# Two rows of a three-product matmul in one instruction of 512 columns, in the feed-forward and pool input blocks

## The reference, cut to what matters

```python
f = rms_norm(h, g_ffn_pre[l])
f = jnp.square(jax.nn.relu(f @ w_ff1[l])) @ w_ff2[l]
h = h + rms_norm(f, g_ffn_post[l])
...
h = _rmsnorm(x, pre_g) * (1 + scale) + shift
proj = h @ w_in
y = _multiscale_pool(proj[..., :POOL_WIDTH], pool_w, pool_scale) * jax.nn.silu(proj[..., POOL_WIDTH:])
x = x + gate * _rmsnorm(y @ w_out, post_g)
```

## Time and profile before

| | |
|---|---|
| median of 3 runs | 1908.66 us (1908.66 to 1909.58) |
| the profiled execution | 1913.2 us, its span 1911.5 us |
| mean granted clock of PE | 0.985 |
| PE busy | 1840.2 us, 11620 matmuls |
| PE weight loads busy | 1663.0 us |
| DVE busy | 1437.2 us |
| ACT busy | 885.8 us |
| POOL busy | 117.3 us |
| HBM read | 419.14 MB, 221 GB/s over the span |

### The profile page before, as it was taken

The page is one execution under the profiler, slowest core; times in us unless marked ns, Lnnn a source line. Parts: engine busy times, 40 slices in busy tenths (PEclk is TensorE's granted clock), DMA queues, the critical chain, the costliest instruction groups (busy, mean ns, idle before and its releaser), DMA issues.

```text
span 1911.5 us, 29730 instructions
## 1 busy us (share of the span) xinstructions
PE 1840.2 (96%) x11620; PEld 1663.0 (87%) x11620; DVE 1437.2 (75%) x1655; ACT 885.8 (46%) x1146; POOL 117.3 (6%) x217
## 2 busy tenths in 40 slices
PE   6999999999999999999999979998999998999997
PEld 6999978799889988998998868887888787999976
DVE  4799986777777798887888978654677577786854
ACT  5344556454434433443344456423566445444442
POOL 0100000100110000000000000001110000000000
PEclk9999999999999999999999989999999998999998
DMA  7865435957898787777777655644443684778652
GB/s 261 290 193 191 162 134 209 327 163 271 309 311 278 241 279 257 251 248 260 251 260 284 237 202 195 209 170 154 153 146 130 234 282 132 240 227 273 210 176 89
DMA packets 185319, 424.80 MB, mean 222 GB/s; under 512 B 8192, under 2 KB 8576, under 8 KB 183680
## 3 DMA queue, kind: packets, MB, share of 16 engines
q1 hardware_dynamic: 157568, 322.69, 49.7%
q0 software_dynamic: 27648, 100.68, 15.8%
HBM read 419.14 MB, written 4.19 MB: 221 GB/s over the span
## 4 chain that ended last, share of the span: by engine, by line
PE 88%; DVE 7%; DMA 2%; ACT 2%; issue 1%; SPq 0%; DVEq 0%; POOLq 0%; POOL 0%; ACTq 0%
PE acc L1743 13%; PE acc L1744 13%; PE acc L1745 13%; PE acc L1756 13%; PE acc L1757 13%; PE acc L1758 13%; DVE mod_sum L1199 2%; PE aux L1794 2%; DVE w_lo L1010 2%; PE aux L2008 1%; DMA mod_raw<-in_ev_mod_w 1%; PE aux L2024 1%; PE aux L1999 1%; PE acc L2024 1%; PE aux L1758 1%
## 5 line engine op out<-in xcount | busy, mean ns | idle before, releaser
L495 ACT ACTIVATE w_hi<-raw 128x1024 fp32r<-128x1024 f32 x552 | 578.3, 1057 | 720.8 <-PE acc L1745 347.7
L1010 DVE TENSOR_TENSOR w_lo<-raw,w_hi 128x1024 fp32r<-128x1024 f32 x552 | 667.5, 1223 | 265.9 <-ACT w_hi L495 264.3
L1743 PE MATMUL acc<-a_hi,w_hi 128*128 128x256 f32 x2304 | 659.5, 286 | 3.6 <-DVE w_lo L1010 3.2
L1745 PE MATMUL acc<-a_hi,w_lo 128*128 128x256 f32 x2304 | 653.4, 284 | 0.0
L1744 PE MATMUL acc<-a_lo,w_hi 128*128 128x256 f32 x2304 | 653.3, 284 | 0.0
L1743 PEld LDWEIGHTS acc<-a_hi,w_hi 128*128 128x128 f32 x2304 | 443.4, 192 | 5.4 <-DVE w_lo L1010 3.6
L1744 PEld LDWEIGHTS acc<-a_lo,w_hi 128*128 128x128 f32 x2304 | 443.4, 192 | 0.7 <-issue 0.5
L1745 PEld LDWEIGHTS acc<-a_hi,w_lo 128*128 128x128 f32 x2304 | 443.1, 192 | 0.0
L1049 DVE SCALAR_TENSOR_TENSOR mod_sum<-mod_raw,silu_c,mod_sum 128x1024 f32<-128x1024 f32 x240 | 301.4, 1279 | 25.6 <-DMA mod_raw<-in_ev_mod_w 16.2
L1756 PE MATMUL acc<-w_hi,b_hi 128*128 128x512 f32 x768 | 302.0, 393 | 0.0
L1757 PE MATMUL acc<-w_lo,b_hi 128*128 128x512 f32 x768 | 300.0, 391 | 0.0
(11 more groups left out here) (217 smaller groups left out, 1437.8 us busy)
## 6 DMA issues: line engine op xcount, KB each, us to landing
raw<-in_w_ff SPq DMA_DIRECT2D x128, 1024.0 KB, 6.7
mod_raw<-in_ev_mod_w POOLq DMA_DIRECT2D x96, 512.0 KB, 5.1
mod_raw<-in_od_mod_w POOLq DMA_DIRECT2D x96, 512.0 KB, 5.2
raw<-in_w_in SPq DMA_DIRECT2D x40, 1024.0 KB, 5.2
raw<-in_ev_w_in SPq DMA_DIRECT2D x40, 1024.0 KB, 5.2
raw<-in_od_w_in SPq DMA_DIRECT2D x32, 1024.0 KB, 5.6
raw<-in_w_out SPq DMA_DIRECT2D x16, 1024.0 KB, 5.2
raw<-in_ev_w_out SPq DMA_DIRECT2D x16, 1024.0 KB, 6.3
```

The lines of the kernel that those rows point to most:

```text
L495: nc.scalar.activation(w_hi[:, s % SLOTS], raw[:, s // 2, KPS * (s % 2):KPS * (s % 2) + KPS, :], ACT.Copy).then_inc(hi_ready, 1)
L1010: nc.vector.tensor_tensor(w_lo[:, s % SLOTS], raw[:, s // 2, KPS * (s % 2):KPS * (s % 2) + KPS, :], w_hi[:, s % SLOTS].bitcast(F32), ALU.s ...
L1743: nc.tensor.matmul(o, wh, hi[:, k, :], start=first and t == 0 and f % 2 == 0, stop=False, skip_group_check=True)
L1745: last = nc.tensor.matmul(o, wl, hi[:, k, :], start=False, stop=t == KPS - 1, skip_group_check=True)
```

## The change

`a_hi` and `a_lo` become the halves of one tensor `a_pair`. `wide_step` does high and low rows in one matmul with the high weights, 512 columns into one bank, and then low weights x high rows, 256 columns into the bank's second half. A 512-column block takes four banks: hidden blocks, `odu` and `odg` use banks 0 to 3 and 4 to 7 in turn; outer blocks take two banks of the eight each. The halves are added on reading: ACT copies the low halves into `hid`, `u_low` or `silu_g`, DVE adds the high halves from PSUM. The relu, and the silu of the gate, then read the sum. `b_lo` of a hidden block is made in the next block's first place. `sum_mod` of od_shift and ev_shift moves behind step 3 of groups 2 and 3, and PE's loops over feed-forward blocks are written out. The spread of the modulation's halves is new, and so are `gate_steps`. On POOL the loads of od_scale for row tiles 7 and 8 go behind `stage_q(0, 0)`. The diff, cut (ACT and DVE runs of `split_hi` move step 4 of a block behind the low copy):

```diff
-        a_hi = sb("a_hi", [P, KT, T], F32R)
-        a_lo = sb("a_lo", [P, KT, T], F32R)
+        a_pair = sb("a_pair", [P, 2, KT, T], F32R)
+        a_hi, a_lo = a_pair[:, 0], a_pair[:, 1]
...
-        acc = [ctx.enter_context(nc.psum_tensor(f"acc{i}", [P, 1024], F32)) for i in range(2)]
-        aux = ctx.enter_context(nc.psum_tensor("aux", [P, 4, 512], F32))
+        banks = ctx.enter_context(nc.psum_tensor("banks", [P, 8, 512], F32))
+        aux = banks[:, 4:8, :]
+        two_banks = [banks[:, 2 * i:2 * i + 2, :].rearrange("p a n -> p (a n)") for i in range(4)]
+        acc = two_banks[:2]
+        wide_acc = [banks[:, 0:4, :], aux]
+        wide_high = [w[:, :, 0:T] for w in wide_acc]
+        wide_low = [w[:, :, T:2 * T] for w in wide_acc]
+        def outer_acc(g, bi):
+            return two_banks[bi if g < FF_GROUPS - 1 or bi < 3 else 0]
...
-            load_mod("od_scale", "od", 1, 1, KT // 2 + 1)
+            load_mod("od_scale", "od", 1, 1, KT // 2 - 1)
...
             pool.wait_ge(q_T_ready, 5)
             stage_q(0, 0)
+            load_mod("od_scale", "od", 1, KT // 2 - 1, KT // 2 + 1)
...
+                    n = 4 * g + bi
                     if b > BLOCK["ff"]:
-                        split_hi(b, range(4, 8))
+                        split_hi(b, range(4 if bi == 0 else 5, 8))
                     split_hi(b + 1, range(4))
-                    act.wait_ge(acc_free, 2 + ACC["ff"] + 8 * g + bi + 1)
+                    block_done(b)
+                    if n:
+                        act.wait_ge(hid_ready, n)
+                    nc.scalar.activation(hid, wide_low[bi % 2], ACT.Copy).then_inc(low_out, 1)
+                    split_hi(b + 1, [4])
+                    act.wait_ge(relu_ready, n + 1)
                     nc.scalar.activation(hid, relu, ACT.Square).then_inc(hid_sq, 1)
                     nc.scalar.activation(b_hi[:, 4 * bi:4 * bi + FT, :], relu, ACT.Square).then_inc(hid_hi, 1)
...
-            def spread(p, start, num, den, first, last):
-
-                done = lambda q: min(max(first + (q - start) * num // den, first), last)
+            def spread(p, start, end, total, hidden=1, outer=1):
+                weight = lambda places: sum(hidden if q // 8 % 8 < 4 else outer for q in places)
+                done = lambda q: total * weight(range(start, q)) // weight(range(start, end))
                 return done(p), done(p + 1) - done(p)
...
-                        halves("ev_shift", *spread(p, 80, 5, 12, 0, 32))
...
-                        halves("od_shift", *spread(p, 23, 5, 8, 0, 32))
...
+                        halves("od_shift", *spread(p, 22, 70, 32))
...
+                        halves("ev_shift", *spread(p, 75, 155, 32, 3, 4))
...
+            def hidden_low(n):
+                bi = n % 4
+                dve.wait_ge(hid_hi, n + 1)
+                nc.vector.tensor_tensor(b_lo[:, FT * bi:FT * (bi + 1), :], hid,
+                                        b_hi[:, FT * bi:FT * (bi + 1), :].bitcast(F32), ALU.subtract).then_inc(hid_ready, 1)
+            def ff_beside(g, block):
+                mods = ff_mods(8 * g + block)
+                def go(i):
+                    if i == 0 and 1 <= block <= 4:
+                        hidden_low(4 * g + block - 1)
+                    mods(i)
+                return go
             def ff_hidden(g):
 
                 for bi in range(4):
-                    each_ahead(BLOCK["ff"] + 8 * g + bi, ff_mods(8 * g + bi), 8, 0 if g or bi else 4)
-                    block_done(BLOCK["ff"] + 8 * g + bi)
-                    if not (g or bi):
+                    n = 4 * g + bi
+                    each_ahead(BLOCK["ff"] + 8 * g + bi, ff_beside(g, bi), 8, 0 if n else 4)
+                    dve.wait_ge(low_out, n + 1)
+                    nc.vector.tensor_tensor(relu, wide_high[bi % 2], hid, ALU.add).then_inc(acc_free, 1)
+                    if n == 0:
                         dve.wait_ge(rstd_ready, 1)
-                    nc.vector.scalar_tensor_tensor(relu, acc[bi % 2][:, :].rearrange("p (f t) -> p f t", f=FT), 0.0, rstd_b,
-                                                   ALU.max, ALU.mult).then_inc(acc_free, 1)
-                    dve.wait_ge(hid_hi, 4 * g + bi + 1)
-                    nc.vector.tensor_tensor(b_lo[:, FT * bi:FT * (bi + 1), :], hid,
-                                            b_hi[:, FT * bi:FT * (bi + 1), :].bitcast(F32), ALU.subtract).then_inc(hid_ready, 1)
+                    dve.wait_ge(acc_free, 2 + ACC["ff"] + 8 * g + bi + 1)
+                    nc.vector.scalar_tensor_tensor(relu, relu, 0.0, rstd_b, ALU.max, ALU.mult).then_inc(relu_ready, 1)
...
-                product = acc[bi % 2][:, :].rearrange("p (t n) -> p t n", t=TT)
+                product = outer_acc(g, bi).rearrange("p (t n) -> p t n", t=TT)
...
+                        dve.wait_ge(low_out, 4 * FF_GROUPS + g + 1)
+                        e = nc.vector.tensor_tensor(u_pad[:, :, POOL_PAD:POOL_PAD + T], wide_high[g % 2], u_low, ALU.add)
+                        e.then_inc(acc_free, 1)
...
-            gate_steps = [(1, 0, 1, 0)] * 5 + [(1, 1, 1, 1)] * 2 + [(2, 2, 0, 0)]
+            def gate_sum(n):
+                dve.wait_ge(low_out, 4 * FF_GROUPS + 4 + n + 1)
+                g4 = silu_g[:, FT * n:FT * (n + 1), :]
+                nc.vector.tensor_tensor(g4, wide_high[n % 2], g4, ALU.add).then_inc(g_summed, 1)
+                dve.sem_inc(acc_free, 1)
+            gate_steps = [(1, 1, 1, 0)] * 2 + [(1, 0, 1, 0)] * 2 + [(0, 0, 0, 0)] + [(1, 1, 1, 1)] * 2 + [(2, 2, 0, 0)]
...
-            dve.wait_ge(acc_free, 2 + ACC["pool"])
             for g in range(4):
+                if g == 0:
+                    gate_sum(3)
+                dve.wait_ge(silu_done, g + 1)
...
+            def wide_step(b, s, rows, out):
+                for t in range(KPS):
+                    k = KPS * s + t
+                    for f in range(FT):
+                        wh = w_hi[:, s % SLOTS, t, P * f:P * (f + 1)]
+                        wl = w_lo[:, s % SLOTS, t, P * f:P * (f + 1)]
+                        nc.tensor.matmul(out[:, f, :], wh, rows[:, :, k, :], start=s == 0 and t == 0, stop=False,
+                                         skip_group_check=True)
+                        last = nc.tensor.matmul(out[:, f, T:2 * T], wl, rows[:, 0, k, :], start=False,
+                                                stop=s == STEPS - 1 and t == KPS - 1, skip_group_check=True)
+                return last
+            def wide_product(b, a, region, beside=None):
+                pe.wait_ge(acc_free, a + 1)
+                for s in range(STEPS):
+                    pe.wait_ge(split_done, 8 * b + s + 9)
+                    wide_step(b, s, a_pair, wide_acc[region]).then_inc(step_done, 1)
+                    if beside:
+                        beside(s)
...
+            for g, unit in ((2, "od_shift"), (3, "ev_shift")):
+                def sum_beside(s):
+                    if s == 3:
+                        pe.wait_ge(acc_free, 2 + ACC["ff"] + 8 * g)
+                        sum_mod(unit, 2, g - 2)
+                wide_product(BLOCK["ff"] + 8 * g, ACC["ff"] + 8 * g, 0, sum_beside)
+                pe.wait_ge(mod_cols_ready, g - 1)
+                ff_hidden(g, 1)
+                ff_outer(g, 4 * g, g == FF_GROUPS - 1)
+            sum_mod("ev_scale", 2, 2)
...
-                nc.scalar.activation(silu_g[:, FT * n:FT * (n + 1), :], acc[n % 2][:, :].rearrange("p (f t) -> p f t", f=FT),
-                                     ACT.Silu).then_inc(acc_free, 1)
+                nc.scalar.activation(silu_g[:, FT * n:FT * (n + 1), :], wide_low[n % 2], ACT.Copy).then_inc(low_out, 1)
...
+            def g_silu(n):
+                act.wait_ge(g_summed, n + 1)
+                g4 = silu_g[:, FT * n:FT * (n + 1), :]
+                nc.scalar.activation(g4, g4, ACT.Silu).then_inc(silu_done, 1)
```

114 lines of the change are left out of this document (63 added, 51 removed).

## The result

| | before | after |
|---|---|---|
| median of the runs | 1909.06 us (1908.66 to 1913.25, 5 runs) | 1899.2 us (1890.78 to 1901.72, 5 runs) |
| profiled execution | 1913.2 us, span 1911.5 | 1895.4 us, span 1893.7 |

A forecast was written before the change was run, and what follows sets the result against it. It took PE to be bound by columns plus 13.3 ns a matmul. 20.5 (matmuls) + 8.1 (queue edit) - 1.4 (pool block) - 1.0 (loads) = 26.2 us, so 1882.5 us; range 1876 to 1898.

The forecast's parts named there:

- Columns plus 13.3 ns a matmul: PE's price in feed-forward: its columns plus 13.3 ns for each matmul at any width; only the second can be saved.
- the 20.5: Gain in us from 64 fewer matmuls in each of 24 blocks (16 hidden, 4 odu, 4 odg), 0.853 us a block.
- the seam: Wide matmul's two 256-column runs, 16 KB apart: taken as free; rival: 13.3 ns, no matmul gain, 1902 us, chance 0.08.
- Added work at nothing: Feed-forward blocks: added ACT and DVE work fits beside PE, DVE at 19.3 of 22.19 us hidden, 20.3 of 21.77 outer.
- Modulation loads in the feed-forward part: Denser od_shift loads: margin falls from 0.8 to 0.25 us a buffer turn; cost 0 to 18.6 us, taken as 1.
- Rival (a): Modulation loads set the pace in the denser feed-forward stretch: 7.4 us lost, 1890 us, at worst 1901; chance 0.13.
- The queue edit: POOL, second attention: od_scale loads behind stage_q(0, 0) end PE's wait ahead of head 0; 8.1 us gained, bounds 5.4 to 8.2.
- Rival (d): Second attention: the stage copy doesn't free PE, since something else ends last there; gain 18.1 us, 1890.5 us; chance 0.09.
- The pool block: Gate adds on DVE in the last odg block and later modulation loads delay the chain behind: 1.4 us lost.
- a stall of 1.5 us at the second pool group: Sign in the pool block: PE stalls since bank 2 is now freed by the gate add; inside the 1.4 us.
- Rival (e): Feed-forward pairs: the 256-column matmul waits for the wide one to drain, 0.163 us a pair, 2133 us; chance 0.04.
- Rival (c): Matmul saving is only that of the skill's figure, something else makes the 13.3 ns: gain 9.5 us, 1899 us; chance 0.04.

The follow-up runs named there:

- the run with one contiguous run: Changed kernel with a_pair laid out so the 512-column matmul reads one run of 512 columns, not two of 256: 1899.56 us, ratio 0.9936.
- the unchanged kernel: The changed kernel run once more with nothing edited, against the kernel before: 1901.49 us, ratio 0.9943.
- the kernel with eight and eight first: Mended kernel with eight wide, then eight narrow matmuls in the first step of every 512-column block: 1892.14 us, ratio 0.9895.
- The mended kernel: Changed kernel with gate halves beside pool input as before, and block 29's transfers ahead of SP's wait for the last hidden tile: 1891.41 us, ratio 0.9907.
- four and four first: Mended kernel with four wide, four narrow, four wide, four narrow matmuls in the first step of every 512-column block: 1886.22 us, ratio 0.9868.

## Why the prediction was wrong

**Columns plus 13.3 ns a matmul.** It held for matmuls of one length in a row, and the alternation reaches it only in one of two patterns. 226.7 + 120 = 346.7 ns is seen, in the pool input blocks of the profiled run; in 15 of the 16 feed-forward hidden blocks it was 353.3. That is the first failed step: 15 x 0.43 = 6.4 us of the 20.5, and up to 8 x 0.43 = 3.4 more in an execution that draws it in the pool input blocks. The prediction had the bounds of the wide matmul's form, 226.7 to 240, and asked only about the seam. It took none "because a 256-column run costs its columns alone once started", and as to the seam that was right (the run with one contiguous run). It never priced the change from one length to the other, which no row of before showed: a form whose neighbours are of another length had no row either, and should have had its own bounds.

**Added work at nothing.** The second failed step. The prediction compared DVE's time with PE's in a block ("20.3 of 21.77. It fits") and followed the order through one hidden block. That part nearly held: in the profile of after PE is never idle in a hidden block, and in the unchanged kernel's second profile once, for 0.57 us. What it did not follow was SP's queue at the end of the last hidden block. Before, SP's wait for the last `b_lo` ahead of block 29's transfers already had ACT idle for 4.88 us. After, the transfers came 1.6 to 3.1 us later, 0.6 of it by the moved `b_lo`, and PE lost 2.5 us (with the load's place mended) to 4.3 (the second profile against before). The gate halves beside the pool input were not costed at all: three halves in block 0 and three in block 1 from two buffers gave 5.34 us of wait for DVE and 2.2 to 2.7 us for PE. All that is added was costed at 1.0 + 1.4; with PE no faster it measured 5.4.

**Modulation loads in the feed-forward part.** Rival (a) was looked for in the right mechanism and the wrong place. In g = 0 and 1 PE has no stall from it in the profile of after. In the second profile DVE waits 2.31 us for `mod_raw` in g = 0 (at 440.12), and PE 0.57 us for `w_lo` at 449.49, which may come of it. Denser loads, those of the gate halves, cost time in the pool input blocks.

**The queue edit.** 8.1 us forecast, 8.1 measured by the medians (interval 5.9 to 11.1), with the clock part; in the profiles the second attention became 7.2 us shorter. The mechanism is shown, that the tenth agrees is luck. Rival (d) falls. **The pool block.** A loss of 1.4 us was forecast against the matmuls' gain; from the start of the last pool input block to PE's restart in the output product it is 57.92 us before (to 1819.09) and 58.56 after (1742.69 to 1801.25), 0.6 us longer where the forecast (1.4 lost of 0.85 gained) comes to 0.5. The size was right, the place not: a stall of 1.5 us at the second pool group was forecast, and PE's longest idle time in the pool block is 0.16 us; it waits ahead of the output product, 1.42 us where it was 0.38. **Rival (e)** falls: the 256-column matmul starts 0.23 to 0.24 us behind the wide one, which is busy for 0.39 to 0.40.

**Rival (c)** came out nearest in time, 1899 for a measured 1899.2, but not in its reason. The Trainium skill, "TensorE: Matmul & The Clock Gate", Part 1, gives about 2.5 ns a matmul beyond its columns; the trace does not agree, since in the better pattern the matmul saved is worth its full 13.3 ns, and 6.7 in the other. That 1899 came out is luck: it is what the pattern and the waits left over.

**The sum again.** The second profile of the unchanged kernel (span 1902.4) can be set against that of before (1911.5) part by part; it has the mean clock of 0.986 for 0.985. The four hidden groups are 0.4, 1.7, 1.4 and 1.4 us shorter, the outer blocks of g = 1 and 2 0.5 each (the modulation sums went from them into the hidden ones), the last outer blocks 4.3 longer, the second attention 6.7 shorter, pool input and product 1.7 shorter. What stands ahead is 0.3 shorter, what follows 1.0 longer. That is the 9.1 us between the two spans.

In the prediction's terms: 26.2, less 8.4 for some 19.5 blocks at 353.3 ns a pair, less 4.3 for the last outer blocks, less 2.2 for the wait at the gate halves, less 1.4 for a second attention that gained 6.7 and not 8.1, plus the 1.0 for loads that wasn't lost. About 1.0 more goes in the first step of the feed-forward part, 4.57 us where it was 3.63. That is clock: its granted clock was 0.68 there, and 0.90 before; in the profile of the kernel with eight and eight first the same step took 3.25 us at 0.99. It comes to 9.9, within 1 us of the 9.1.

The two halves of the change alone sum to 8.1 + 5.7 = 13.8 us, and both together gave 9.6 and 9.9. The profile of the half without the queue edit drew 346.7 ns in g = 0 from the second block on and in most pool input blocks, and its last outer blocks took 89.93 us for 91.82. That is enough for the gap, and nothing in it depends on the queue edit, but one profile of each doesn't show that it is so in every run. The mended kernel with four and four first has 25.2 us. So most of what the matmuls were to give exists; the prediction failed on what takes it away.

## What to carry over

A price per matmul taken from rows of equal neighbours doesn't hold for a sequence that alternates lengths; give such a sequence bounds of its own, and try its order, since here the order of one step in eight was worth 5 us. Where a step moves to a later block, follow every queue that waits for its semaphore, the transfers of other blocks among them, and look in the trace of before for how much reserve they have. Count halves against buffers place by place: engine time that fits says nothing of that. And before two profiles are compared stretch by stretch, compare their granted clock in each stretch.

## What the hardware showed unexpectedly

Alternating matmuls of 512 and 256 columns run in one of two steady patterns, 346.7 or 353.3 ns a pair, at a granted clock of 1.00 in both. Each is kept over hundreds of pairs. It changes at a short stall, at a few matmuls of another kind or at another order of a step, and then the same way in g = 2 and g = 3 of one execution. By execution the same code can have either, which is worth up to 3.4 us in the pool input blocks.

The granted clock also fell to 0.50 (1.2 GHz) in places where PE was busy nearly all the time, as for 6.83 us at 1485.34 in the profile of before, and in other executions of kernels with the same code there it did not. That made 2.5 us in the second attention and about 1 us in the first step of the feed-forward part. What brings it on there isn't shown.
